# Last groups of a banded attention: GpSimd scales the probabilities, each turned tile is read by two engines, and the middle keys are turned once

## The chip, the core and the metric

The program runs on one core of a Trainium2 chip. The metric is the device time of one execution in microseconds (us), lower is better. One execution of each kernel was also taken by the hardware profiler; all rows come from it.

## What is computed

A decoder trunk of two layers, for 512 prompt tokens and 8 sample tokens. The change is in the token mixer of the second layer, attention of 16 heads (4 key heads) in blocks of 128 queries. Each query sees the block of keys before its own and its own block, within a band, and a learned sink takes part in the sum of each row:

```python
band = (diff >= 0) & (diff <= WINDOW)            # WINDOW = 128
s = jnp.where(mask[None, :, None, None], s, -jnp.inf)
p = sink_probs(s, sinks).astype(v.dtype)         # exp(s - mx) / (sum + exp(sink - mx))
o = jnp.einsum('bnkgqs,bnskd->bnqkgd', p, vc).reshape(B, T, SW_HEADS * SW_HD)
return o @ w_out, k[:, T - nkeep:], v[:, T - nkeep:]
```

## The kernel before

The program is written by hand: five instruction streams (TensorE, VectorE, ScalarE, GpSimd, SyncE) in a fixed order, which meet only at semaphores. An instruction that waits holds up all that stands behind it on its engine. Most of the time is dense products: a weight tile is split into a high and a low part (ScalarE writes `wH`, VectorE writes `wL`), and TensorE makes three products of each.

The attention is cut into 16 groups `gi` (4 sets of heads by 4 query blocks; `gi % 4 == 0` is the first block, which has no keys before it and so about two thirds of the work). Each group makes this round:

1. `window_scores(gi)`, TensorE: scores into the PSUM tile `tile`, four rows of 192 keys and a sink for each query.
2. `shift(gi)`, VectorE: minus the maximum of each row, into `sm`.
3. `exps(gi)`, ScalarE: four exponentials with their sums, into an SBUF buffer `soft`.
4. `normalise(gi)`, VectorE: reciprocal of the sums, then four multiplications, in place. The semaphore `s_norm` rises after the second and after the fourth.
5. `turn(gi)`, TensorE: transposes of 128 by 128 into the PSUM tile `side`, half 0 after the first rise of `s_norm`, half 1 after the second. In this buffer the two rows of a half are 257 wide with zeros where a row has no keys; the middle 128 keys of the two rows are turned one after the other and added up in PSUM, so that a half takes four transposes (two in a first block). GpSimd writes the zeros beforehand (`clear_between`).
6. `turn_read(gi)`: copy of `side` into SBUF `softT`. For groups 0 to 3 ScalarE reads half 0 and VectorE half 1, for groups 4 and 5 VectorE reads both, from group 6 on ScalarE reads both.
7. `weigh(gi)`, TensorE: turned probabilities by values, into `sums` (group 15: into `tile[0]`).
8. `att_high(gi)` on ScalarE and `att_low(gi)` on VectorE: the high and the low part of the result, `xH` and `xL`, which the output product `sout` reads.

Groups 0 to 4 run between the chunks of the product `qkv` (up to about 770 us of the trace), groups 5 to 15 without such cover, one behind the other (770 to 803 us). There TensorE's order is `window_scores(gi + 2)`, `turn(gi)`, `weigh(gi - 1)`; ScalarE's is `exps(gi + 1)`, `turn_read(gi)`, `att_high(gi - 1)`; VectorE's is `shift(gi + 1)`, `normalise(gi)`, `att_low(gi - 2)`. In group 7 VectorE also makes two products of the rotation of the last queries and in group 8 their sum (`rope_sum`), and in the last two groups TensorE makes `sample_scores` where `window_scores` would stand. Behind `weigh(15)` TensorE goes on with `sout`. TensorE waits before `window_scores(gi)` until `exps(gi - 2)` is done, before `turn(gi)` until `side` has been read, and before `weigh(gi)` until its turned tile has been copied.

## Time and profile before

| | |
|---|---|
| median of 3 runs | 1303.2 us (1303.16 to 1304.3) |
| profiled execution, its own time | 1304.2 us |
| its span in the trace | 1302.4 us |
| TensorE matmuls busy | 1290.9 us, 99% |
| VectorE / ScalarE / GpSimd busy | 888.9 / 593.4 / 73.7 us |
| granted TensorE clock, mean | 0.997 of full speed |

A row of the timeline gives the start, the time from the start of the first to the end of the last of its instructions, the engine, line, operation, output and inputs, the number of instructions, and in brackets the time that the engine stood idle before and what ended it. Ends of matmuls are modelled and overlap the next ones, so that the pace of TensorE is read from the distance between two starts.

### The profile page before, as it was taken

The numbers are of one execution on the slowest core, as the hardware profiler recorded it, in microseconds if no ns is written. First come the engines' busy times: TensorE is split into PE (matmuls) and PEld (weight loads), VectorE is DVE, ScalarE is ACT, GpSimd is POOL, SyncE is SP. The second block draws the span as 40 slices with busy tenths as digits, with TensorE's granted clock in tenths as the row PEclk, the third lists the DMA queues.
The fourth block names the chain that finished last, engine by engine and source line by source line (L and its number), as shares of the span: only waits on it lengthen the run. The fifth ranks groups of instructions, "written<-read, shape, count | busy, mean of one in ns | idle before, by whom it ended". The sixth has DMA issues, their size and how long they took to land.

```text
span 1302.4 us, 25274 instructions
## 1 busy us (share of the span) xinstructions
PE 1290.9 (99%) x10790; PEld 1257.8 (97%) x10790; DVE 888.9 (68%) x1597; ACT 593.4 (46%) x1059; POOL 73.7 (6%) x115
## 2 busy tenths in 40 slices
PE   9998999999999999999999999999999999999998
PEld 8998989999999999999999988999999999999998
DVE  7897876987777774223897787698777777422385
ACT  6213555544444442222754767555444444322371
POOL 1121330000000000000031010000000000000000
PEclk9998999999999999999999999999999999999999
DMA  5436622213323224221414232311323323322231
GB/s 199 155 97 189 227 81 82 91 42 97 96 83 98 94 92 135 90 90 62 146 51 151 77 98 80 98 66 49 98 82 98 95 85 110 113 90 92 77 129 66
DMA packets 35409, 131.84 MB, mean 101 GB/s; under 512 B 4469, under 2 KB 5085, under 8 KB 35009
## 3 DMA queue, kind: packets, MB, share of 16 engines
q1 hardware_dynamic: 29520, 111.33, 26.5%
q0 software_dynamic: 5344, 18.26, 4.3%
q8 instruction: 85, 1.39, 0.4%
q10 hardware_dynamic: 432, 0.64, 0.2%
q14 instruction: 28, 0.22, 0.1%
HBM read 121.26 MB, written 10.08 MB: 101 GB/s over the span
## 4 chain that ended last, share of the span: by engine, by line
PE 94%; DVE 2%; ACT 2%; DMA 1%; issue 0%; ACTq 0%; DVEq 0%
PE tile L1174 24%; PE tile L1176 24%; PE tile L1178 24%; PE tile L1184 4%; PE tile L1185 4%; PE tile L1186 4%; PE tile L1646 1%; PE side L1184 1%; DMA raw<-in_w_qo 1%; PE side L1185 1%; PE side L1186 1%; ACT xH L780 0%; DMA raw<-in_w_kv 0%; PE sums L1345 0%; DVE wL L1829 0%
## 5 line engine op out<-in xcount | busy, mean ns | idle before, releaser
L753 ACT ACTIVATE wH<-raw 128x1024 fp32r<-128x1024 f32 (+1 forms) x190 | 210.7, 1112 | 384.8 <-DMA raw<-in_w_up 145.6
L1174 PE MATMUL tile<-xH,wH 128*128 128x260 f32 x1798 | 363.7, 283 | 0.0
L1178 PE MATMUL tile<-xH,wL 128*128 128x260 f32 x1798 | 363.0, 284 | 0.0
L1176 PE MATMUL tile<-xL,wH 128*128 128x260 f32 x1798 | 362.6, 283 | 0.0
L1829 DVE TENSOR_TENSOR wL<-raw,wH 128x1024 fp32r<-128x1024 f32 (+1 forms) x190 | 245.8, 1295 | 159.7 <-ACT wH L753 155.6
L1174 PEld LDWEIGHTS tile<-xH,wH 128*128 128x128 f32 x1798 | 278.0, 189 | 3.9 <-issue 3.4
L1178 PEld LDWEIGHTS tile<-xH,wL 128*128 128x128 f32 x1798 | 278.0, 189 | 0.0
L1176 PEld LDWEIGHTS tile<-xL,wH 128*128 128x128 f32 x1798 | 277.4, 189 | 0.0
L1877 DVE SCALAR_TENSOR_TENSOR u<-tile,rstd 128x520 f32<-128x520 f32 x96 | 67.1, 699 | 121.7 <-PE tile L1178 121.6
L1174 PE MATMUL tile<-hidH,wH 128*128 128x260 f32 x616 | 124.3, 283 | 0.0
L1178 PE MATMUL tile<-hidH,wL 128*128 128x260 f32 x616 | 123.8, 282 | 0.0
L1176 PE MATMUL tile<-hidL,wH 128*128 128x260 f32 x616 | 123.8, 282 | 0.0
L1184 PE MATMUL tile<-xH,wH 128*128 128x260 f32 x400 | 116.0, 290 | 0.1
L1185 PE MATMUL tile<-xL,wH 128*128 128x260 f32 x400 | 113.1, 283 | 0.0
L1186 PE MATMUL tile<-xH,wL 128*128 128x260 f32 x400 | 112.8, 282 | 0.0
L1176 PEld LDWEIGHTS tile<-hidL,wH 128*128 128x128 f32 x616 | 95.1, 188 | 0.0
L1178 PEld LDWEIGHTS tile<-hidH,wL 128*128 128x128 f32 x616 | 94.9, 188 | 0.0
L1174 PEld LDWEIGHTS tile<-hidH,wH 128*128 128x128 f32 x616 | 94.8, 188 | 0.0
L1184 PEld LDWEIGHTS tile<-xH,wH 128*128 128x128 f32 x400 | 75.3, 188 | 2.7 <-issue 2.3
L1185 PEld LDWEIGHTS tile<-xL,wH 128*128 128x128 f32 x400 | 75.3, 188 | 0.3
L1186 PEld LDWEIGHTS tile<-xH,wL 128*128 128x128 f32 x400 | 75.3, 188 | 0.0
L974 ACT ACTIVATE cv<-u,taps 128x520 f32<-128x520 f32 x44 | 36.2, 823 | 48.8 <-DVE u L1877 48.4
(445 smaller groups left out, 1909.3 us busy)
## 6 DMA issues: line engine op xcount, KB each, us to landing
raw<-in_w_up SPq DMA_DIRECT2D x88, 512.0 KB, 3.6
raw<-in_w_down SPq DMA_DIRECT2D x32, 704.0 KB, 4.1
raw<-in_w_ple SPq DMA_DIRECT2D x16, 512.0 KB, 5.9
raw<-in_w_qo SPq DMA_DIRECT2D x12, 512.0 KB, 3.6
raw<-in_w_qkv SPq DMA_DIRECT2D x12, 512.0 KB, 3.6
raw<-in_w_kv SPq DMA_DIRECT2D x10, 512.0 KB, 3.7
cring<-in_c_in POOLq DMA_DIRECT2D x8, 512.0 KB, 4.7
out_c_s<-cring POOLq DMA_DIRECT2D x8, 512.0 KB, 3.2
```

The source lines that it names most:

```text
L753: nc.scalar.activation(wH[j][:, 0:n], raw[j][:, 0:n], ACT.Copy).then_inc(s_high, 1)
L974: nc.scalar.activation(dst[:], u[:, r, 2:], ACT.Identity, bias=taps[:, r, 3:4], scale=taps[:, r, 2:3]).then_inc(s_ca, 1)
L1174: nc.tensor.matmul(out[:, q, 0:HT], wh, x[0][:, k, tokens(q)], start=first, stop=False)
L1176: nc.tensor.matmul(out[:, q, 0:HT], wh, x[1][:, k, tokens(q)], start=False, stop=False)
L1178: mm = nc.tensor.matmul(out[:, q, 0:HT], wl, x[0][:, k, tokens(q)], start=False, stop=last)
L1184: nc.tensor.matmul(out, wh, x[0][:, k, tokens(q)], start=first, stop=False)
L1185: nc.tensor.matmul(out, wh, x[1][:, k, tokens(q)], start=False, stop=False)
L1186: return nc.tensor.matmul(out, wl, x[0][:, k, tokens(q)], start=False, stop=last)
L1646: nc.tensor.matmul(banks[half][:, e, at0 + 2 * HD - HD * m + k0:at0 + 3 * HD], queries[r, gp, m * P:m * P + P], qk[r, gp // 2, k0:HD * m + ...
L1829: nc.vector.tensor_tensor(wL[j][:, 0:n], raw[j][:, 0:n], wH[j][:, 0:n].bitcast(F32), ALU.subtract).then_inc(s_low, 1)
L1877: nc.vector.scalar_tensor_tensor(out=halves(dst), in0=bank(stage, c)[0:rows, :, 0:HT], scalar=scale, in1=halves(rstd[0:rows, :]), op0=ALU. ...
```

## The change

- The buffer `soft` loses the zeros between its two rows. The last 64 keys of the first row stand beside the first 64 of the second, so that three transposes turn a half (in a first block two, of which one is 64 columns wide). `clear_between` and its semaphore are gone. This holds for all 16 groups.
- From group 8 on (`SPREAD`) the four multiplications of `normalise` run on GpSimd (`scale`); VectorE keeps the reciprocal.
- From group 8 on ScalarE reads half 0 of the turned tile and VectorE half 1. `soft_late` has three places where it had two, and `exps` waits for the `turn` of three groups before, where it was two.

```diff
@@ -55,6 +55,7 @@
 BOTH = 6
+SPREAD = 8
 QUERIED = 6
@@ -277,13 +278,13 @@
         sw = Region(xH_at + KT // 2 * T * 4)
-        soft_early = sw("soft_early", [P, 2, 4, 2 * P + 1])
+        soft_early = sw("soft_early", [P, 2, 2, 2 * (3 * HD + 1)])
         assert sw.top <= xL_at
         sw = Region(xL_at + KT // 2 * T * 4)
         softT_early = sw("softT_early", [P, 2, 2, 3 * P])
         assert sw.top <= xL_at + KT * T * 4
         sw = Region(arena + size([P, KT, T]))
-        soft_late = sw("soft_late", [P, 2, 4, 2 * P + 1])
+        soft_late = sw("soft_late", [P, 3, 2, 2 * (3 * HD + 1)])
         softT_late = sw("softT_late", [P, 2, 2, 3 * P])
@@ -437,11 +439,24 @@
 
-            return (soft_early if gi < BESIDE else soft_late)[:, gi % 2]
+            return soft_early[:, gi % 2] if gi < BESIDE else soft_late[:, gi % 3]
+
+        def soft_row(gi, c):
+            at0 = c % 2 * (3 * HD + 1)
+            return soft_of(gi)[:, c // 2, at0:at0 + 3 * HD + 1]
 
         def softT_of(gi):
 
             return (softT_early if gi < BESIDE else softT_late)[:, gi % 2]
+
+        def scale(eng, gi):
+            lo = first_key(gi)
+            for c in range(4):
+                at0 = 1 if c % 2 == 0 and gi % 4 else 0
+                keys = soft_row(gi, c)[:, at0 + lo:at0 + 3 * HD]
+                step = eng.tensor_scalar(keys, keys, sm[:, gi % 2, 1, c:c + 1], None, ALU.mult)
+                if c % 2:
+                    step.then_inc(s_norm, 1)
 
@@ -467,7 +482,7 @@
         def both_on_act(gi):
-            return gi >= BOTH
+            return BOTH <= gi < SPREAD
 
@@ -475,6 +490,10 @@
             return gi + 1 - sum(both_on_dve(n) for n in range(gi + 1))
+
+        def turned_by_dve(gi):
+
+            return gi + 1 - sum(both_on_act(n) for n in range(gi + 1))
 
@@ -571,23 +590,16 @@
                     .to_broadcast([P, NQ // 2, 2, HD])))
-            clear_between(soft_early)
             assert made.n == MADE
 
         def last_rotation(pool):
             pool.wait_ge(s_mm, CHUNK0["qkv"] + COUNT["qkv"])
-            clear_between(soft_late)
             pool.wait_ge(s_read, READ0["qkv"] + LASTQ + 1)
             pool.wait_ge(s_rotr, LASTQ - 3)
             half = HD // 2
             for i in range(4):
                 pool.dma_start(rotated[half * i:half * i + half, LASTQ % 2, :],
                                u[half * (i ^ 1):half * (i ^ 1) + half, LASTQ % 2, 0:T]).then_inc(s_rotl, 16)
-
-        def clear_between(soft):
-            for e, column in enumerate((3 * HD + 1, 0)):
-                mm = nc.gpsimd.memset(soft[:].rearrange("p k (i e) t -> p (k i) e t", e=2)[:, :, e, column:column + HD], 0.0)
-            mm.then_inc(s_swk, 1)
 
@@ -735,6 +747,10 @@
                     nc.gpsimd.memset(acc[:], 0.0).then_inc(s_acc, 1)
+                    for gi in range(SPREAD, 4 * NB):
+                        pool.wait_ge(s_norm, 2 * gi)
+                        pool.wait_ge(s_inv, gi - SPREAD + 1)
+                        scale(nc.gpsimd, gi)
                     pool.wait_ge(s_rope, 2 + KT)
@@ -1099,12 +1115,14 @@
                 act.wait_ge(s_z, gi + 1)
-                if gi >= 2:
+                if 2 <= gi < BESIDE:
                     act.wait_ge(s_tu, 2 * (gi - 1))
+                if gi >= BESIDE + 3:
+                    act.wait_ge(s_tu, 2 * (gi - 2))
                 k = gi % 2
                 for c in range(4):
                     last = nc.scalar.activation(
-                        soft_of(gi)[:, c, w.start + HD * (c % 2):w.stop + HD * (c % 2)], score_tile(gi)[:, c // 2, :].rearrange("p (c s) -> p c s", c=2)[:, c % 2, w],
+                        soft_row(gi, c)[:, w], score_tile(gi)[:, c // 2, :].rearrange("p (c s) -> p c s", c=2)[:, c % 2, w],
                         ACT.Exp, bias=sm[:, k, 0, c:c + 1], accum_out=sm[:, k, 1, c:c + 1])
@@ -1662,30 +1680,23 @@
                     pe.wait_ge(s_tua, turned_by_act(gi - 1))
-                    pe.wait_ge(s_tud, min(gi, BOTH))
-                if gi == 0:
-                    pe.wait_ge(s_swk, 1)
-                if gi == BESIDE:
-                    pe.wait_ge(s_swk, 2)
+                    pe.wait_ge(s_tud, turned_by_dve(gi - 1))
                 soft = soft_of(gi)
                 for half in range(2):
                     pe.wait_ge(s_norm, 2 * gi + half + 1)
-                    earlier, later = soft[:, 2 * half, :], soft[:, 2 * half + 1, :]
-                    nc.tensor.transpose(side[:, half, 2 * P:3 * P], later[:, P:2 * P], ident)
                     if gi % 4 == 0:
-                        mm = nc.tensor.transpose(side[:, half, P:2 * P], earlier[:, P:2 * P], ident)
+                        mm = nc.tensor.transpose(side[0:HD, half, P:2 * P], soft[:, half, P:P + HD], ident)
                     else:
-                        nc.tensor.transpose(side[:, half, 0:P], earlier[:, 1:1 + P], ident)
-                        nc.tensor.matmul(side[:, half, P:2 * P], later[:, 0:P], ident, is_transpose=True,
-                                         start=True, stop=False, skip_group_check=True)
-                        mm = nc.tensor.matmul(side[:, half, P:2 * P], earlier[:, 1 + P:1 + 2 * P], ident, is_transpose=True,
-                                              start=False, stop=True, skip_group_check=True)
+                        for i in range(2):
+                            mm = nc.tensor.transpose(side[:, half, i * P:i * P + P], soft[:, half, 1 + i * P:1 + i * P + P],
+                                                     ident)
+                    mm = nc.tensor.transpose(side[:, half, 2 * P:3 * P], soft[:, half, 1 + 2 * P:1 + 3 * P], ident)
                     mm.then_inc(s_tu, 1)
 
             def weigh(gi):
                 gp, n = divmod(gi, 4)
                 pe.wait_ge(s_tua, turned_by_act(gi))
-                pe.wait_ge(s_tud, min(gi + 1, BOTH))
+                pe.wait_ge(s_tud, turned_by_dve(gi))
                 if 1 <= gi < 4 * NB - 1:
@@ -2509,16 +2520,13 @@
             def normalise(gi):
-                k = gi % 2
-                lo = first_key(gi)
                 dve.wait_ge(s_soft, gi + 1)
-                chain.link(nc.vector.reciprocal(sm[:, k, 1, :], sm[:, k, 1, :]))
-                for c in range(4):
-                    at0 = HD if c % 2 else 1 if gi % 4 else 0
-                    keys = soft_of(gi)[:, c, at0 + lo:at0 + 3 * HD]
-                    step = nc.vector.tensor_scalar(keys, keys, sm[:, k, 1, c:c + 1], None, ALU.mult)
-                    if c % 2:
-                        step.then_inc(s_norm, 1)
+                inverse = nc.vector.reciprocal(sm[:, gi % 2, 1, :], sm[:, gi % 2, 1, :])
+                if gi < SPREAD:
+                    chain.link(inverse)
+                    scale(nc.vector, gi)
+                else:
+                    inverse.then_inc(s_inv, 1)
 
@@ -2583,6 +2591,8 @@
                     normalise(gi)
+                if gi > SPREAD:
+                    turn_read(gi - 1)
                 if gi == BESIDE:
@@ -2598,6 +2608,7 @@
             att_low(groups - 2)
+            turn_read(groups - 1)
             att_low(groups - 1)
```

The program order shows where the new copy stands in VectorE's stream. These are VectorE's rows from the reciprocal of group 15 on, before: the multiplications, `att_low(13)`, the step for the samples, `wL`, then `att_low(14)` and `att_low(15)`.

```order
L2515 RECIPROCAL sm<-sm 128x4
L2519 TENSOR_SCALAR soft_late<-soft_late,sm 128x192 x4
L2535 TENSOR_TENSOR xL<-sums,xH 128x2x128
L2461 TENSOR_REDUCE sst<-tile 128x1
L2462 TENSOR_TENSOR sst<-sst 128x1
L2463 TENSOR_TENSOR sst<-sst 128x1
L1829 TENSOR_TENSOR wL_53<-raw_54,wH_52 128x1024
L2535 TENSOR_TENSOR xL<-sums,xH 128x2x128
L2535 TENSOR_TENSOR xL<-tile,xH 128x2x128
```

And the same place of the changed program, where the two copies of `side` are `turn_read(14)` and `turn_read(15)`:

```order
L2524 RECIPROCAL sm<-sm 128x4
L2537 COPY softT_late<-side 128x384
L2543 TENSOR_TENSOR xL<-sums,xH 128x2x128
L2472 TENSOR_REDUCE sst<-tile 128x1
L2473 TENSOR_TENSOR sst<-sst 128x1
L2474 TENSOR_TENSOR sst<-sst 128x1
L1840 TENSOR_TENSOR wL_53<-raw_54,wH_52 128x1024
L2543 TENSOR_TENSOR xL<-sums,xH 128x2x128
L2537 COPY softT_late<-side 128x384
L2543 TENSOR_TENSOR xL<-tile,xH 128x2x128
```

The copy of group 15's half 1 stands between the two last `att_low`, behind the one of group 14. On GpSimd, the rows between the rotation of the last queries and the first step of the next layer were these:

```order
L584 DMA rotated<-u 32x520 x4
L737 MEMSET acc 128x520
L739 MEMSET u 128x512
L713 DMA convw<-in_convw 128x176
L714 DMA prev<-in_conv_prev 128x704
```

They are now:

```order
L601 DMA rotated<-u 32x520 x4
L749 MEMSET acc 128x520
L457 TENSOR_SCALAR soft_late<-soft_late,sm 128x128 x4
L457 TENSOR_SCALAR soft_late<-soft_late,sm 128x192 x12
L457 TENSOR_SCALAR soft_late<-soft_late,sm 128x128 x4
L457 TENSOR_SCALAR soft_late<-soft_late,sm 128x192 x12
L755 MEMSET u 128x512
L725 DMA convw<-in_convw 128x176
L726 DMA prev<-in_conv_prev 128x704
```

The 32 multiplications of groups 8 to 15 stand ahead of a fill and of two loads for the next layer. On TensorE a first block (here group 0) was turned by four equal transposes:

```order
L1674 MATMUL side<-const,soft_early 128x128
L1676 MATMUL side<-const,soft_early 128x128
L1674 MATMUL side<-const,soft_early 128x128
L1676 MATMUL side<-const,soft_early 128x128
```

In the changed program every second one is 64 wide:

```order
L1688 MATMUL side<-const,soft_early 64x128
L1693 MATMUL side<-const,soft_early 128x128
L1688 MATMUL side<-const,soft_early 64x128
L1693 MATMUL side<-const,soft_early 128x128
```

Four transposes stay four here; in the twelve other groups eight become six.

## Rows read from the trace of the kernel before

**Rows 1.** The page: TensorE's busy time, and the chain that ended last.

```profile
PE 1290.9 (99%) x10790; PEld 1257.8 (97%) x10790; DVE 888.9 (68%) x1597; ACT 593.4 (46%) x1059; POOL 73.7 (6%) x115
...
PE 94%; DVE 2%; ACT 2%; DMA 1%; issue 0%; ACTq 0%; DVEq 0%
```

**Rows 2.** Windows, busy time of PE, PEld, DVE, ACT, POOL in five us.

```profile
785.00:790.00 5.00, 4.82 (x57) 3.57 (x56) 4.50 (x17) 5.00 (x22) 0.00 (x0) 1.00 0.15 58
```

**Rows 3.** Timeline of PE, one full round in the late groups.

```profile
788.60 0.92 PE L1646 MATMUL tile<-qk 64*128 64x192 f32 x8
...
789.69 0.27 PE L1674 MATMUL side<-const,soft_late 128*128 128x128 f32 x1
789.80 0.27 PE L1678 MATMUL side<-const,soft_late 128*128 128x128 f32 x1
...
790.66 0.44 PE L1697 MATMUL sums<-softT_late,vst 128*64 128x128 f32 x4
...
791.63 0.92 PE L1646 MATMUL tile<-qk 64*128 64x192 f32 x8
```

**Rows 4.** Timeline of PE, where it stood idle in the late groups.

```profile
773.66 0.44 PE L1697 MATMUL sums<-softT_late,vst 128*64 128x128 f32 x4 [0.24 <-issue]
...
780.92 0.30 PE L1674 MATMUL side<-const,soft_late 128*128 128x128 f32 x1 [0.21 <-DVE soft_late L2519]
...
785.83 0.71 PE L1646 MATMUL tile<-qk 64*128 64x64 f32 x8 [0.18 <-ACT soft_late L1106]
```

**Rows 5.** Timeline of PE, a `weigh` after dense products.

```profile
768.83 0.40 PE L1178 MATMUL tile<-pxH,wL 128*128 128x260 f32 x2
769.16 0.44 PE L1697 MATMUL sums<-softT_early,vst 128*64 128x128 f32 x4
```

**Rows 6.** Timeline of POOL, the only multiplications by a scalar column.

```profile
679.62 2.92 POOL L563 TENSOR_SCALAR partsB<-partsB,sinks 128x8 bf16<-128x8 bf16 x3
```

**Rows 7.** Timeline of DVE in the same stretch.

```profile
681.00 0.76 DVE L2349 SCALAR_TENSOR_TENSOR pxL<-h,front,pxH 128x520 fp32r<-128x520 f32 x1 [0.19 <-ACT pxH L1058]
681.67 0.69 DVE L2342 TENSOR_TENSOR cv<-gate_more,pwo 128x520 f32<-128x520 f32 x1
```

**Rows 8.** POOL by source line: shortest, median and longest ns.

```profile
L563 POOL TENSOR_SCALAR partsB<-partsB,sinks x3: 598/852/1284, 679.6 to 681.9; 128x8 bf16<-128x8 bf16 x3
...
L571 POOL CAST bandB<-const x2: 1041/1393/1745, 699.1 to 700.8; 128x1024 bf16<-128x1024 f32 x2
...
L609 POOL TENSOR_TENSOR prob<-prob,kvq x4: 997/1010/1023, 140.5 to 179.2; 128x384 f32<-128x384 f32 x4
```

**Rows 9.** Timeline of DVE, the steps of groups 8 and 15.

```profile
780.09 0.17 DVE L2515 RECIPROCAL sm<-sm 128x4 f32<-128x4 f32 x1
...
781.49 0.68 DVE L2421 TENSOR_TENSOR qk<-cg,cv 128x512 f32<-128x512 f32 x1
...
799.16 0.18 DVE L2515 RECIPROCAL sm<-sm 128x4 f32<-128x4 f32 x1 [1.19 <-ACT soft_late L1106]
799.37 1.01 DVE L2519 TENSOR_SCALAR soft_late<-soft_late,sm 128x192 f32<-128x192 f32 x4
```

**Rows 10.** Timeline of PE, the end of the attention.

```profile
800.16 0.33 PE L1674 MATMUL side<-const,soft_late 128*128 128x128 f32 x1
...
801.18 0.44 PE L1697 MATMUL sums<-softT_late,vst 128*64 128x128 f32 x4
...
802.15 0.44 PE L1697 MATMUL tile<-softT_late,vst 128*64 128x128 f32 x4
...
803.12 0.39 PE L1184 MATMUL tile<-xH,wH 128*128 128x260 f32 x1
```

**Rows 11.** Timeline of ACT, the end of the attention.

```profile
802.29 0.38 ACT L1124 ACTIVATE xH<-sums 128x256 fp32r<-128x256 f32 x1 [0.18 <-PE sums L1708]
```

**Rows 12.** Timeline of DVE, its last steps, and an early half copy.

```profile
761.29 0.55 DVE L2529 COPY softT_early<-side 128x384 f32<-128x384 f32 x1
...
802.70 0.42 DVE L2535 TENSOR_TENSOR xL<-sums,xH 128x256 fp32r<-128x256 f32 x1 [0.27 <-ACT xH L1124]
```

5 lines of the change are left out of this document (3 added, 2 removed).

## The prediction

> **What bounds the kernel now.** I read the page first. TensorE is busy 99% of the span and the chain that ended last lies on it for 94% [rows 1]: whatever is taken off TensorE's stream counts at once, unless TensorE then waits for something else, and a wait that it did not have before counts in full. GpSimd has nothing to do for 94% of the time.
>
> Then the windows of the late groups. From 785 to 790 us TensorE and ScalarE both show 5.00 of 5 us, VectorE 4.50 [rows 2]. So there are three nearly full engines, and a round of a group passes through all of them.
>
> Then TensorE's timeline. One full round runs from 788.60 to 791.63, 3.03 us: scores 1.09, `turn` 0.97 (from 789.69 to 790.66), `weigh` 0.97. The transposes start 0.11 us apart (789.69, 789.80), though each shows 0.27 [rows 3]: the price of a transpose is 0.11. The stream does not run without gaps. It stood before `weigh(5)` (for VectorE's copy), before `turn(8)` (for VectorE's multiplications) and before `window_scores(12)` (for ScalarE's exponentials of group 10) [rows 4]. At these three places a transpose saved ahead of the gap only makes the gap longer.
>
> **The change part by part.**
>
> Transposes. 24 of them go (12 groups, one in each half), 24 x 0.11 = 2.64 us. In groups 1, 2 and 3 dense products stand around them and TensorE waits for nothing: 6 x 0.11 = -0.66. Group 5's two are lost in the gap before `weigh(5)`, those of 6 and 7 in the gap before `turn(8)`, those of 9 in the gap before `window_scores(12)` [rows 4]. Left are groups 10, 11, 13, 14 and 15, each -0.22, if GpSimd keeps up (below).
>
> The 64-wide transpose. No row of before has one. The nearest: between two dense products of `qkv` TensorE goes on every 0.12 us, so the pair at 768.83 should be followed at 769.07; `weigh`, whose weights are 64 wide, starts at 769.16 [rows 5], 0.09 later. In a first block the widths now go 128, 64, 128, 64, 128, four changes where there was none. Below: nothing, as the load of a narrow tile might be free when the output is a transpose. Above: 0.09 for each of four, 0.36 a group. I take 0.3, as every `weigh` shows the gap: groups 0, 4 and 12, +0.9; in group 8 it lies in a wait. The Trainium skill has a rule here, in TensorEngine Tiling, Key Properties: changing the tiling mode drains TensorE. By it all four changes cost, as by the row; without it the sum would be 0.9 lower.
>
> GpSimd's multiplication. VectorE takes 1.01 us for its four (799.37) [rows 9], about 0.24 each. GpSimd's price is the term that decides most. Its only multiplications by a scalar column are three of 8 elements, and they took 598 to 1284 ns, 2.92 us together [rows 6, 8]. Taken as a fixed cost this would be about 0.97 each. But at the same time VectorE ran instructions with two inputs in SBUF: one from 681.00 to 681.76, the next from 681.67 to 682.36 [rows 7], and GpSimd's last one ended at 682.54, 0.18 behind it. I read the three as blocked by VectorE, and not as slow. A conversion of 1024 elements with one input took 1.04 us at its best [rows 8], so 1.0 ns an element at most; 192 elements give 0.20, and with about 0.1 for the start 0.30. Below: 0.20, that rate with no start. Above: the product of two tensors of 384 elements took 1.01 us [rows 8], 2.6 ns an element, so 0.50; above that again the 0.97 of the three. I take 0.30, from the row that has one input as these have. The Trainium skill's GPSIMD Engine Reference says in Key points that VectorE is about twice as fast in elementwise work; by that the price would be near 0.5 and the sum that of the slow rival below. No row here shows it for one input.
>
> What GpSimd's price does. `turn(gi)` starts when the first two products are there and its second half when all four are. Two products take 0.6, TensorE's half of a `turn` now takes 0.37: where TensorE stands right behind GpSimd, its second half waits 0.22, just what the two transposes saved.
> - Group 8. The reciprocal is at 780.09 [rows 9], GpSimd starts near 780.3, and its four short products (128 elements, 0.2 each) are ready at 781.1 if nothing blocks them. But VectorE's `rope_sum`, two inputs in SBUF, 0.68 us (781.49 before) [rows 9], is now due near 780.4, since the four products no longer stand ahead of it. It and the third product collide, and `turn(8)` ends up to 0.6 later. `weigh(7)` started right behind `turn(8)` before. Bounds -0.1 and +0.7; I take +0.2, as half the products are through by then.
> - Group 10 follows the wait for ScalarE at 785.83 [rows 4]: behind `exps(10)` come one score step on TensorE (0.84) and, beside it, reciprocal, hop, two products, hop: 0.1 + 0.15 + 0.6 + 0.2 = 1.05, and the second half after that. TensorE stands behind GpSimd; +0.1.
> - Group 11: -0.2. Group 13: -0.2.
> - Groups 14 and 15. The stream of TensorE holds less here. For 15 the reciprocal came at 799.16 [rows 9] and `turn` at 800.16 [rows 10]; 799.16 + 1.05 = 800.2. So what was gained before is lost here, and the second half waits: together +0.2.
>
> The copy of group 15. This is the term I am surest of. Before, `weigh(15)` started at 802.15, at once behind `weigh(14)` [rows 10]. Now it needs `turn_read(15)` of VectorE, which stands behind `att_low(14)`, which needs `att_high(14)` of ScalarE, which needs the end of `weigh(14)`. The times of this chain are in the rows: `weigh(14)` ends at 802.15, `att_high(14)` starts at 802.29 [rows 11], `att_low(14)` at 802.70 [rows 12] and gives way 0.33 later, at 803.03; the copy of half a turned tile takes 0.55 (761.29) [rows 12], to 803.58; 0.1 of hop. `weigh(15)` starts at 803.68 in place of 802.15: +1.5. Behind it stands all of `sout`, whose first product was at 803.12 [rows 10], on the same engine. Nothing covers it. ScalarE's shorter copy and the third place of `soft_late` cannot help here; elsewhere they take off load from ScalarE, which is full [rows 2], and I give them no price, as TensorE's waits are for GpSimd then.
>
> The other moves on GpSimd, the fill for the samples and two loads, go from 783 us to after 801. They are used only within and after `sout`: +0. The removed zero fills: 0, nothing waited for them.
>
> Sum: -0.66 + 0.9 + 0.2 + 0.1 - 0.2 - 0.2 + 0.2 + 1.5 = +1.8 (group 12 is in the 0.9). On the profiled execution's own 1304.2 this gives 1306.0, its span 1302.4 becoming 1304.2; that execution was 1.0 above the median of the runs, 1303.2, on which I predict: 1305.0 us.
>
> **The rivals.**
>
> *Faster.* If the narrow transpose is free, GpSimd needs 0.2 or less and `rope_sum` does not collide, TensorE is the bound throughout: -2.64 + 0.22 (group 5) + 1.5 = -0.9, and the gaps before `turn(8)` and `window_scores(12)` close, -0.4: 1301.9. For it speaks that VectorE and ScalarE are both relieved; against it that ScalarE's exponentials, not its copies, set the pace of group 10, and that GpSimd's rate in the rows gives 0.20 only with no start. To pass 0.2% the copy of group 15 would have to be hidden as well, and the order of the stream excludes that.
>
> *Slower, GpSimd as the bound.* At 0.36 to 0.40 for a product the second halves start to wait in every group, since two products are then longer than the 0.37 and the round's slack is used up. At 0.5 the second half of `turn` waits 0.6 in groups 10, 14 and 15 and some 0.2 to 0.6 in the others; walking the round through with 0.5 I get +4.5 in place of +1.8, 1307.7. At 0.97 GpSimd's 3.9 us a group against a round of 2.8 rules all eight: about +18, 1321. For it speak the three rows taken at their face; against, the match of their ends with VectorE's.
>
> *Slower, the lock.* The Trainium skill says the same of two-input instructions, in SBUF — State Buffer, Who interferes with whom. The trace agrees in the three rows. As a mechanism of this kernel it strikes once, in group 8, at +0.7 rather than +0.2: 1305.5.
>
> **How the numbers follow.** My forecast, with the lock in group 8 either way, 1303.7 to 1306.4: 0.52. The faster rival with its milder forms, 1301 to 1303.7: 0.15. GpSimd between 0.36 and 0.6, 1306.4 to 1311: 0.27. GpSimd near 0.97: 0.06. The range takes in the first three but for their tails: 1302.3 to 1308.8. A measurement of this kernel can tell about 0.2%, 2.6 us, from no change, so "slower" begins at 1305.8: all of the slow cases and a tenth of mine, 0.33 + 0.05 = 0.38. "Faster" ends at 1300.6: 0.04. The rest, 0.58, is no change that can be told.
>
> **What the new profile would show.** Right: `weigh(15)` idle for some 1.5 us behind `weigh(14)`, released by VectorE's copy; GpSimd's products about 0.3 us apart; a gap of near 0.1 at each narrow transpose; the second half of `turn` behind GpSimd in groups 10, 14 and 15. Wrong: products 0.5 apart or more (slow rival), `turn(8)` no later than before (no collision), or narrow transposes 0.11 apart on both sides (that term is nothing).

## The result, and the profile after

The changed kernel takes 1317.3 us (median of 4 runs, 1316.35 to 1318.12), the kernel before 1303.4 beside it (1303.16 to 1304.3). The ratio is 1.0104, with a 95% interval of 1.0092 to 1.0116: by it the kernel is 13.6 us slower (the two medians lie 14.0 apart). The forecast of 1305.0 had foreseen 1.8 us, and its range ended at 1308.8.

The page of the changed kernel, the lines that answer to [rows 1]:

```profile
PE 1294.0 (98%) x10766; PEld 1257.1 (96%) x10766; DVE 886.0 (67%) x1573; ACT 592.2 (45%) x1059; POOL 95.6 (7%) x143
...
PE 90%; DVE 4%; ACT 2%; POOL 2%; DMA 1%; issue 1%; ACTq 0%; DVEq 0%; POOLq 0%
```

TensorE's share of the chain that ended last fell from 94% to 90%, and GpSimd is now in it. GpSimd's own timeline shows why:

```profile
779.65 2.55 POOL L457 TENSOR_SCALAR soft_late<-soft_late,sm 128x128 f32<-128x128 f32 x4 [7.06 <-DVE sm L2524]
783.51 2.99 POOL L457 TENSOR_SCALAR soft_late<-soft_late,sm 128x192 f32<-128x192 f32 x4 [1.31 <-DVE sm L2524]
787.82 2.99 POOL L457 TENSOR_SCALAR soft_late<-soft_late,sm 128x192 f32<-128x192 f32 x4 [1.31 <-DVE sm L2524]
...
804.26 6.08 POOL L457 TENSOR_SCALAR soft_late<-soft_late,sm 128x192 f32<-128x192 f32 x8 [1.31 <-DVE sm L2524]
```

Four products of a full group take 2.99 us, 0.75 each, where I had taken 0.30 and VectorE needed 1.01 for all four [rows 9]. And GpSimd then stands idle for 1.31 us before it may begin the next group, so that two scalings start 4.31 us apart (783.51 to 787.82), against a round of 3.03 before [rows 3]. It waits for the reciprocal of VectorE, and VectorE's timeline says what that waited for:

```profile
786.61 0.96 DVE L2518 TENSOR_REDUCE sm<-tile 128x4 f32<-128x772 f32 x1 [1.61 <-POOL soft_late L457]
787.49 0.17 DVE L2524 RECIPROCAL sm<-sm 128x4 f32<-128x4 f32 x1
787.57 0.53 DVE L2537 COPY softT_late<-side 128x384 f32<-128x384 f32 x1
```

GpSimd ends group 9 at 783.51 + 2.99 = 786.50; `shift(11)` starts at 786.61, `reciprocal(10)` behind it in VectorE's order at 787.49, GpSimd's group 10 at 787.82. The list of waits in the late groups (us in total, times, the longest) names the two halves of this ring. Of the first, 7.1 us lie ahead of GpSimd's first group and do not belong to it:

```profile
POOL soft_late L457 <- DVE sm L2524: 14.8, 7, 7.1
...
DVE sm L2518 <- POOL soft_late L457: 10.1, 6, 2.1
```

`shift(gi + 1)` waits for `s_norm` of group `gi - 1`. Before, VectorE had raised that semaphore itself, and the wait was over when it came to it. Now it is GpSimd's, the reciprocal of group `gi` stands behind it, and GpSimd's next scaling needs that reciprocal: scaling, `shift`, reciprocal, scaling, and none of these steps overlaps another.

TensorE's timeline shows the waits, where [rows 4] had three of 0.18 to 0.24:

```profile
781.18 0.27 PE L1688 MATMUL side<-const,soft_late 128*64 128x128 f32 x1 [1.37 <-POOL soft_late L457]
782.25 0.30 PE L1688 MATMUL side<-const,soft_late 128*64 128x128 f32 x1 [0.69 <-POOL soft_late L457]
...
790.87 0.44 PE L1691 MATMUL side<-const,soft_late 128*128 128x128 f32 x2 [0.87 <-POOL soft_late L457]
...
812.31 0.70 PE L1708 MATMUL sums<-softT_late,vst 128*64 128x128 f32 x4
...
815.44 0.44 PE L1708 MATMUL tile<-softT_late,vst 128*64 128x128 f32 x4 [1.53 <-DVE softT_late L2537]
...
816.41 0.39 PE L1202 MATMUL tile<-xH,wH 128*128 128x260 f32 x1
```

And its windows (the window's length, then the busy time of PE, PEld, DVE, ACT and POOL in it, then TensorE's granted clock). The first five are five us long, the last two lie inside them and are one us long:

```profile
780.00:785.00 5.00, 3.12 (x26) 2.10 (x28) 2.33 (x5) 2.36 (x9) 3.69 (x7) 0.79 0.00 0
785.00:790.00 5.00, 4.29 (x37) 2.66 (x33) 2.53 (x7) 4.48 (x19) 3.69 (x6) 0.87 0.02 5
790.00:795.00 5.00, 3.22 (x32) 1.98 (x32) 1.74 (x4) 2.73 (x11) 3.80 (x6) 1.00 0.00 0
...
805.00:810.00 5.00, 3.22 (x26) 2.02 (x30) 0.91 (x3) 1.86 (x10) 4.91 (x8) 0.68 0.00 0
810.00:815.00 5.00, 3.92 (x38) 2.58 (x33) 2.76 (x7) 1.22 (x3) 2.02 (x5) 0.64 0.33 90
...
784.00:785.00 1.00, 1.00 (x10) 0.98 (x8) 0.42 (x1) 0.84 (x2) 1.00 (x3) 0.50 0.00 0
...
808.00:809.00 1.00, 1.00 (x9) 0.72 (x8) 0.56 (x1) 0.00 (x0) 1.00 (x3) 0.50 0.00 0
```

Where [rows 2] had three engines nearly full, VectorE is now busy about half the time, and at two places the granted clock fell to 0.50, the lower level of 1.2 GHz, after TensorE had stood still.

To compare single executions I use the stage from the first transpose of group 0 to the first product of `sout`: before 733.35 to 803.12 [rows 10], 69.77 us; changed 733.36 to 816.41, 83.05 us. The stage holds +13.28 us, nearly all of the difference. What lies behind the stage, to the end of the span, takes 499.2 to 499.3 us in the profiled execution of every kernel here but two (e2 and f7, below), so that the stage says nearly all there is to say.

### The profile page after: what moved, and what is told of

Read it like the earlier page. It is cut to its first block, busy times and chain, and to the rows that moved or that the text cites. A ratio compares the mean times of both kernels' runs of the same rounds, so it can differ in the third digit from the quotient of the medians.

```text
span 1315.7 us, 25241 instructions
## 1 busy us (share of the span) xinstructions
PE 1294.0 (98%) x10766; PEld 1257.1 (96%) x10766; DVE 886.0 (67%) x1573; ACT 592.2 (45%) x1059; POOL 95.6 (7%) x143
## 4 chain that ended last, share of the span: by engine, by line
PE 90%; DVE 4%; ACT 2%; POOL 2%; DMA 1%; issue 1%; ACTq 0%; DVEq 0%; POOLq 0%
PE tile L1192 23%; PE tile L1196 23%; PE tile L1194 23%; PE tile L1202 4%; PE tile L1203 4%; PE tile L1204 4%; POOL soft_late L457 2%; DMA raw<-in_w_qo 1%; DVE wL L1840 1%; PE side L1202 1%; PE side L1203 1%; PE side L1204 1%; PE tile L1664 1%; ACT xH L796 0%; DVE cv L1873 0%
```

## Experiments

Times are medians. The ratio is to the kernel before on the same chip in the same job; the medians of the kernel before lie between 1303.1 and 1303.9 in these jobs, so kernels of different jobs are compared by their ratios. "Stage" is the stretch defined above, in us, from one execution.

| kernel | us | ratio and interval | stage |
|---|---|---|---|
| changed | 1317.32 | 1.0104, 1.0092 to 1.0116 | 83.05 |
| e1: VectorE scales | 1304.9 | 1.0010, 1.0000 to 1.0019 | 71.63 |
| e2: ring opened | 1312.08 | 1.0069, 1.0056 to 1.0083 | 78.11 |
| e3: turned once only | 1302.05 | 0.9989, 0.9980 to 0.9998 | 68.03 |
| e4: copy of 15 earlier | 1315.1 | 1.0090, 1.0076 to 1.0104 | 81.24 |
| f1: filler on TensorE | 1314.35 | 1.0090, 1.0076 to 1.0103 | 80.91 |
| f4: price list on e3 | 1303.69 (1 run) | | 69.49 |
| f5: e3, group 5 on ScalarE | 1301.3 | 0.9990, 0.9981 to 0.9998 | 68.14 |
| f6: half on each engine | 1304.15 | 1.0009, 1.0000 to 1.0018 | 70.65 |
| f7: product of two tensors | 1308.17 | 1.0039, 1.0025 to 1.0052 | 73.51 |
| f8: f7, ring opened, copy early | 1305.82 | 1.0020, 1.0011 to 1.0029 | 72.56 |
| f9: copies alone | 1304.07 | 1.0004, 0.9995 to 1.0013 | 70.88 |
| g1: f8 without shared copies | 1306.18 | 1.0019, 1.0010 to 1.0028 | 72.03 |

### The three parts apart

**e1**, the change with the scaling put back on VectorE:

```diff
-                    for gi in range(SPREAD, 4 * NB):
-                        pool.wait_ge(s_norm, 2 * gi)
-                        pool.wait_ge(s_inv, gi - SPREAD + 1)
-                        scale(nc.gpsimd, gi)
...
-                if gi < SPREAD:
-                    chain.link(inverse)
-                    scale(nc.vector, gi)
-                else:
-                    inverse.then_inc(s_inv, 1)
+                chain.link(inverse)
+                scale(nc.vector, gi)
```

> The changed kernel with one part undone: VectorE makes the four multiplications of all 16 groups again, GpSimd none; the shared reading of the turned tile, the three places of soft_late and the transposes stay as changed. Theory A (GpSimd's multiplications, 0.75 us each, make up nearly all of the loss; at the end remains the copy of group 15, 1.5 us): +0.5 to +2.5 us on the kernel before, 1304 to 1306, and no window of the late groups with a lower granted clock. Rival B (the loss is in the split reading and in the narrow transposes): above +6.

Measured 1304.9, granted clock 1.00 in all windows. The stage is 11.42 us shorter than the changed kernel's: GpSimd's scaling, with all that it brings, is that much of the 13.28. The waits that stay are for VectorE's copy, in TensorE's timeline:

```profile
783.76 0.41 PE L1687 MATMUL side<-const,soft_late 128*128 128x128 f32 x2 [0.76 <-DVE softT_late L2530]
...
804.05 0.44 PE L1704 MATMUL tile<-softT_late,vst 128*64 128x128 f32 x4 [1.52 <-DVE softT_late L2530]
```

**e2**, the ring opened; GpSimd scales as in the change:

```diff
@@ exps(gi)
+                if gi >= 2:
+                    act.wait_ge(s_norm, 2 * (gi - 1))
@@ shift(gi)
-                    dve.wait_ge(s_norm, 2 * (gi - 1))
+                    dve.wait_ge(s_soft, gi - 1)
```

> The changed kernel; VectorE's row maximum (shift) of a group no longer waits until the group two before has been scaled, ScalarE's exponentials wait for that instead (they are what overwrites the sums). GpSimd's work is the same. Theory A1 (the round of 4.3 us is a ring: GpSimd's scaling 3.0, then shift 0.9 and reciprocal on VectorE, then the next scaling, so that GpSimd stands idle 1.3 us in each group): the idle time of GpSimd goes, the distance of two groups' scalings falls from 4.3 to 3.1 to 3.9 us, and the time falls by 3 to 7 us, to 1310 to 1314. Rival A2 (GpSimd's price alone sets the round): no more than 1 us less, 1316 to 1318.

1312.08, the stage 4.94 us shorter. GpSimd's timeline now has scalings much closer to each other:

```profile
796.02 2.98 POOL L457 TENSOR_SCALAR soft_late<-soft_late,sm 128x192 f32<-128x192 f32 x4 [0.74 <-DVE sm L2526]
799.15 2.98 POOL L457 TENSOR_SCALAR soft_late<-soft_late,sm 128x192 f32<-128x192 f32 x4 [0.15 <-POOL soft_late L457]
```

799.15 - 796.02 is 3.13 us, GpSimd's own price and little more. Not all of GpSimd's idle time went: between its first and its last scaling it is 4.4 us in place of 7.7, and the longest that is left is this one:

```profile
785.95 6.05 POOL L457 TENSOR_SCALAR soft_late<-soft_late,sm 128x192 f32<-128x192 f32 x8 [2.00 <-DVE sm L2526]
```

From the first scaling's start to the last one's it takes 24.41 us (778.34 to 802.75), in the changed kernel 27.7 (779.65 to 807.3, halfway through the row of eight). So the ring itself is worth 3.3 us of the 4.94. Another 1.5 lie behind the last scaling, where the changed kernel's clock was low. In e2 it fell later: the windows from 809 to 812 us show 0.56, 0.50 and 0.50, `sout` starts within them at 810.26, and what lies behind the stage takes 500.3 us, 1.1 more than elsewhere. The ring is real, and it is less than half of what GpSimd costs.

**e3**, the kernel before with the middle keys turned once (the edit is to the changed kernel). The three places of `soft_late`, and the looser wait of `exps` that goes with them, do not depend on `SPREAD` and stay in:

```diff
-SPREAD = 8
+SPREAD = 16
...
-            turn_read(groups - 1)
```

> The kernel before with only the packed buffer and its transposes (24 fewer, and 8 narrow ones): VectorE scales everywhere, ScalarE reads both halves from group 6 on. Theory C (a transpose is 0.11 us on TensorE, a narrow one costs as a wide one, and five late groups as well as three early ones are bound by TensorE): -1.0 to -2.3 us, 1301.0 to 1302.4. Rival D (ScalarE sets the round of the late groups, so that a saved transpose is waited for there): -0.3 to -0.9 us, from the early groups alone.

1302.05, faster than the changed kernel and, by 0.1% with an interval that stays below 1, than the one before. The stage is 1.74 us shorter than before. Whether the third place has any part in that is not shown; the transposes alone were predicted to give 1.76 (below).

**e4**, the two last copies exchanged:

```diff
-            att_low(groups - 2)
             turn_read(groups - 1)
+            att_low(groups - 2)
             att_low(groups - 1)
```

> The changed kernel with VectorE's copy of group 15 moved ahead of att_low(14). Theory E (weigh(15) waits 1.5 us for that copy alone, and all of sout stands behind it): 1.2 to 1.6 us less than the changed kernel, 1315.7 to 1316.2, and weigh(15) starts right behind weigh(14). Rival F (the weights of sout or the granted clock hold the end): the wait moves to the first products of sout, under 0.4 us less.

1315.1, by the ratios 1.8 us less than the changed kernel and so a little more than the 1.2 to 1.6 that were expected. TensorE's row of `weigh(15)` shows no wait any more, and the stage is 1.81 us shorter.

**f9**, e1 with the exchange of e4. It differs from e3 by the shared copies alone, since e3 has the third place too (against what was written down before the run):

> VectorE scales all groups, the middle keys are turned once, each turned tile from group 8 on is read half by ScalarE and half by VectorE, three places, and group 15's is read ahead of att_low(14). So it differs from the kernel with the middle keys turned once only by the shared copies and the third place. Theory (ScalarE's load was not what TensorE waited for, so that sharing the copy is worth nothing, and VectorE, 4.50 of 5 us busy, pays for it): 1302.3 to 1304, 0 to 2 us behind the 1302.05 of the kernel with the middle keys turned once only. Rival (sharing pays once its tail is gone): below 1301.5, and this would be the version to keep.

1304.07, 2.0 us behind e3 by the ratios, the stage 2.85 behind. Most of it is that `turn(gi + 1)` has to wait until VectorE has read its half, and that copy stands behind VectorE's four products. VectorE's and then TensorE's timeline:

```profile
784.00 1.01 DVE L457 TENSOR_SCALAR soft_late<-soft_late,sm 128x192 f32<-128x192 f32 x4
784.93 0.55 DVE L2530 COPY softT_late<-side 128x384 f32<-128x384 f32 x1
```

```profile
785.58 0.41 PE L1687 MATMUL side<-const,soft_late 128*128 128x128 f32 x2 [0.38 <-issue]
```

The row says "issue", but the copy ends at 785.48, 0.10 before the transpose starts. The tail is not gone either. Ahead of the copy of group 15 now stands VectorE's `wL`, and `weigh(15)` still waits 0.76 us. VectorE's rows and TensorE's:

```profile
800.40 1.22 DVE L1836 TENSOR_TENSOR wL<-raw,wH 128x1024 fp32r<-128x1024 f32 x1
801.53 0.55 DVE L2530 COPY softT_late<-side 128x384 f32<-128x384 f32 x1
```

```profile
802.23 0.44 PE L1704 MATMUL tile<-softT_late,vst 128*64 128x128 f32 x4 [0.76 <-DVE softT_late L2530]
```

So the exchange that gave 1.81 us in the changed kernel gives 0.75 here (stages of e1 and f9).

### The price of a GpSimd multiplication

**f4**, on e3, in a stretch where GpSimd has nothing else to do:

```diff
+                    tried = Chain(pool, sem("tried"))
+                    for n in (8, 64, 192, 288):
+                        for _ in range(3):
+                            tried.link(nc.gpsimd.tensor_scalar(scratch[:, 0:n], const[:, 0:n], eps[:, 0:1], None, ALU.mult))
...
+                            tried.link(nc.gpsimd.tensor_scalar(scratch[:, 0:n], const[:, 0:n], 2.0, None, ALU.mult))
...
+                            tried.link(nc.gpsimd.tensor_copy(scratch[:, 0:n], const[:, 0:n]))
...
+                        tried.link(nc.gpsimd.tensor_tensor(scratch[:, 0:192], const[:, 0:192], const[:, 0:192], ALU.mult))
```

> A price list, on the kernel with the middle keys turned once and nothing else changed. GpSimd makes 30 instructions on a scratch tile in a stretch where it has nothing else to do, each behind the one before: three each of a multiplication by a column for 8, 64, 192 and 288 elements a row, by a constant for 8 and 192, a copy of 8 and of 192, a product of two tensors of 192. Theory B (the price belongs to the instruction): the multiplication by a column costs 0.29 us and 2.5 ns an element, so 0.31, 0.45, 0.77 and 1.01 us. Theory D (the start is dear, and the size counts little): the three before the change, 598 to 1284 ns for 8 elements, were the true price, so all sizes near 0.6 to 0.9. For the kind: if the column is what costs, the constant takes 0.3 us or less at 192 and the copy about 0.3 (1 ns an element, as the conversions of 1024 elements in 1.04 us before the change); if all operations of this width run at one rate, constant and copy also take 0.7 to 0.8. The product of two tensors: 0.78 (2.6 ns an element plus the start). The time of the kernel should be that of its base, 1302 +- 1, as nothing waits for these.

The groups by shape (busy us, mean ns of one, idle us before), and one instruction each of the two larger column sizes from GpSimd's timeline:

```profile
L754 POOL TENSOR_SCALAR scratch<-const,eps 128x8 f32<-128x8 f32 x3 | 0.9, 311 | 0.2
...
L757 POOL TENSOR_SCALAR scratch<-const 128x192 f32<-128x192 f32 x3 | 2.2, 733 | 0.2
...
L760 POOL COPY scratch<-const 128x192 f32<-128x192 f32 x3 | 1.0, 342 | 0.2
...
L762 POOL TENSOR_TENSOR scratch<-const 128x192 f32<-128x192 f32 x3 | 1.5, 506 | 0.2
```

```profile
775.22 0.76 POOL L754 TENSOR_SCALAR scratch<-const,eps 128x192 f32<-128x192 f32 x1
...
780.65 1.00 POOL L754 TENSOR_SCALAR scratch<-const,eps 128x288 f32<-128x288 f32 x1
```

The shortest of three each, 0.31, 0.76 and 1.00 for 8, 192 and 288 elements, lie on 0.29 us and 2.5 ns an element, as expected. With 64 the shortest was 0.44, which fits too. VectorE worked beside them, and some took longer: one of 192 took 0.87 (776.08), one of 288 took 1.52 (777.90). A constant is hardly cheaper than a column (0.69 at its best); a copy of the same size takes 0.34, close to my 0.30; and what I had not expected, the product of two tensors takes 0.51 and is cheaper than the product with one. The kernel's time was to stay that of e3; the one run and the stage (+1.46) say that it did not. The likely cause is in VectorE's rows. Its four products took 1.01 us in e3 and up to 1.43 beside GpSimd, and TensorE waited for them three times before a `turn` (0.61, 0.26 and 0.19 us), in e3 once (0.32):

```profile
788.66 1.43 DVE L458 TENSOR_SCALAR soft_late<-soft_late,sm 128x192 f32<-128x192 f32 x4
```

**f7**, the change with the other form on GpSimd:

```diff
+                    step = eng.tensor_tensor(keys, keys, inverse.to_broadcast([P, 3 * HD - lo]), ALU.mult)
```

> The changed kernel, but GpSimd scales with a product of two tensors, the second being the column of inverse sums repeated along the row, in place of the multiplication by a column. In the price list a GpSimd product of two tensors of 192 took 0.51 us, the multiplication by a column 0.76 for the same 192. Theory P (the form sets GpSimd's price, and the price and the ring set the loss): four products take 2.05 us in place of 2.99, the distance of two scalings falls from 4.3 us by 0.94 to 3.36 (idle of GpSimd still 1.3), and seven rounds give 6 to 6.6 us back, less where TensorE's own round of 2.8 takes over: 1311 to 1312.5. Rival Q (a repeated column is no cheaper than the column form): the four take 2.8 us or more and the time stays at 1316 to 1318. Rival R (two inputs in SBUF collide with VectorE's att_low and rope work and slow both): four take 2.3 to 2.6 and VectorE's two-input rows grow, 1313 to 1315.5.

1308.17, 3 us better than the best that was expected. GpSimd's timeline:

```profile
788.37 1.89 POOL L461 TENSOR_TENSOR soft_late<-soft_late,sm 128x192 f32<-128x192 f32 x4 [1.15 <-DVE sm L2528]
791.56 1.47 POOL L461 TENSOR_TENSOR soft_late<-soft_late,sm 128x128 f32<-128x128 f32 x4 [1.29 <-DVE sm L2528]
```

The mechanism of theory P holds: four products 1.89 instead of 2.99, starts 3.19 apart, GpSimd's idle time nearly as it was. From the first scaling to the last it took 21.42 us (778.54 to 799.96), in the changed kernel 27.7 (779.65 to 807.3, halfway through the row of eight): 6.2 us less, as expected. Of the 9.54 us by which the stage is shorter the rest was left out of the expectation: the last scaling counts too (1.1), and the clock stayed at 1.00 from 775 to 805 us (2.1 by f1). But it fell right behind the stage, where `sout` had started at 805.90:

```profile
805.00:810.00 5.00, 5.00 (x37) 4.66 (x38) 2.37 (x6) 1.07 (x5) 0.00 (x0) 0.66 0.67 240
```

What lies behind the stage takes 500.9 us here, 1.6 more than elsewhere. So most of what the stage saved on the clock was paid later, and the whole kernel is 8.5 us faster than the changed one by the ratios.

**f8** is f7 with the edits of e2 and e4.

> The same, and with it the ring opened (shift waits for the exponentials of two groups before, the exponentials wait for the scaled probabilities) and group 15's turned tile read ahead of att_low(14). GpSimd's 2.05 us a group is then below the round of 2.8 us, and nothing of VectorE waits for it. Theory: what is left is latency, two products of 1.0 us before each half of turn where VectorE needed 0.5, so up to 0.5 us a group where TensorE stands right behind; 1303 to 1307. By my prediction's walk with 0.5 us a product the kernel would be at 1307.7 with the copy of group 15 unhidden, 1306.1 with it hidden. Rival S (GpSimd's work itself, by slowing VectorE and ScalarE or by one more hop in the chain of each group, costs what the price list does not show): 1308 or more.

1305.82, inside the expected range and 2.6 us over before by the ratio. TensorE's waits name what is left: 2.5 us in all for GpSimd's scaling (1.46 of them in group 8, then 0.19 to 0.32 in four groups) and 0.39 before `weigh(15)` for VectorE's copy. That is the latency of a slower engine in the chain of each group; between its groups GpSimd itself stands idle again.

**f6**, the dose between: VectorE scales rows 0 and 1, GpSimd rows 2 and 3 beside it, with a semaphore of its own, and the edits of e2 and e4:

```diff
+                    dve.wait_ge(s_inv, gi - SPREAD + 1)
+                    scale(nc.vector, gi, (0, 1))
...
-                        scale(nc.gpsimd, gi)
+                        scale(nc.gpsimd, gi, (2, 3))
```

> The dose between none and four GpSimd products a group. From group 8 on VectorE scales rows 0 and 1 and GpSimd rows 2 and 3, beside each other behind the same reciprocal, with a semaphore of its own for GpSimd's half; shift waits for the exponentials of two groups before in place of the scaled probabilities, and group 15's turned tile is read ahead of att_low(14). Theory (GpSimd's 0.75 us a product and the ring are the whole loss): two products take 1.5 us, well below the round of 2.8 us, so GpSimd bounds nothing; the first half of turn starts as in the kernel before, the second 0.9 us after it in place of 0.37, so up to 0.5 us a group where TensorE stands right behind, less where it has slack. With the copy of group 15 costing nearly nothing now: 1302.5 to 1305.5. Rival (any GpSimd work there slows VectorE through SBUF, VectorE being busy 4.50 of 5 us): VectorE's multiplications and att_low get longer by 20% or more, and the time is 1307 or more.

1304.15, as the theory had it, and the first half of the rival is true as well. The two engines slow each other: VectorE's two products take 0.72 (four took 1.01 alone, so two about 0.5), GpSimd's two 1.63 (1.52 by the price list):

```profile
795.28 0.72 DVE L463 TENSOR_SCALAR soft_late<-soft_late,sm 128x192 f32<-128x192 f32 x2
```

`att_low` did not get longer (0.41), and the time stayed 3 us below the rival's. Against f9, which differs by the scaling and its waits, f6 is the same within its interval.

**g1** has f8's scaling, and ScalarE reads the whole turned tile as before the change:

```diff
-SPREAD = 8
+SPREAD = 16
+GPS = 8
...
-                    for gi in range(SPREAD, 4 * NB):
+                    for gi in range(GPS, 4 * NB):
...
-            turn_read(groups - 1)
```

> Middle keys turned once; from group 8 on GpSimd scales with the product of two tensors, the ring is open, three places; but the turned tiles are read whole by ScalarE, as before the change, so no copy of VectorE stands in any round from group 6 on. It differs from the kernel with two-input form and open ring (1305.8) by the shared copies alone, and from the one with the middle keys turned once only (1302.05) by GpSimd's scaling alone. Theory (the shared copy costs some 2 us wherever it is, since VectorE's half stands behind other work and the next turn waits for it): 1303 to 1304.3, and GpSimd's scaling itself costs 1 to 2 us by its latency. Rival U (with VectorE relieved of its multiplications the shared copy is no longer late there, so sharing costs nothing and ScalarE's whole copy now waits instead): 1305 to 1306.5. Rival V (with VectorE relieved and ScalarE's order unchanged this is the best form): below 1301.5.

1306.18 against f8's 1305.82, stages 72.03 and 72.56: rival U, with the median inside its range and the interval's reach of 1 us around it. Where VectorE no longer multiplies, its half of the copy is not late in the rounds; sharing costs nothing there that the runs can tell and brings nothing. The stages differ by 0.53, of which 0.39 is f8's wait before `weigh(15)`. So the price of sharing depends on what VectorE has ahead of the copy.

### The clock

**f1**, products that nobody reads, in front of TensorE's waits:

```diff
                 for half in range(2):
+                    for _ in range(0 if gi < SPREAD else 3 if half else {8: 5, 10: 3, 13: 1, 14: 4}.get(gi, 0)):
+                        nc.tensor.matmul(side[:, half, 3 * P:4 * P], ones, ident, start=True, stop=True)
```

> Question: how much of the changed kernel's loss is TensorE's clock? In its trace the granted clock is 0.79 and 0.87 of full speed from 780 to 790 us and 0.68 and 0.64 from 805 to 815 us, stretches in which TensorE stood waiting before; elsewhere it is 1.00. This kernel is the changed one with products of ones by the unit matrix put in front of TensorE's waits (three ahead of the second half of each turn from group 8 on, five ahead of the first half in group 8, three in group 10, one in 13, four in 14), written to columns of side that nobody reads; they use up time in which TensorE stood. Theory F (the clock is the rest): walking the late groups through with 0.75 us for a GpSimd product gave +11.2 of the +13.3 us between the first transpose and the first product of sout, and the early transposes -0.6, so that some 2.6 us are left for the clock. Then the granted clock is 1.00 or near it in these windows, turn and window_scores take 1.1 us there in place of 1.5 to 2.0, and the time falls by 1.5 to 2.8 us against the changed kernel, to 1314.5 to 1315.8. Rival G (the slow TensorE instructions were hidden in the wait for GpSimd): the clock rises and the time stays within 0.6 us, 1316.7 to 1317.9, since the round is GpSimd's 3.0 us and the 1.3 us between its groups. Rival H: the filler stands in the way, each product of it behind an unfinished wait, and the time rises by 1 us or more.

1314.35, 1.8 us less than the changed kernel by the ratios; the stage is 2.14 us shorter. Windows of f1 at the two places:

```profile
780.00:785.00 5.00, 4.40 (x43) 3.03 (x43) 1.84 (x5) 2.83 (x10) 3.69 (x6) 1.00 0.01 2
...
805.00:810.00 5.00, 4.73 (x58) 3.74 (x58) 1.88 (x7) 2.19 (x8) 4.91 (x8) 1.00 0.00 0
```

GpSimd's timeline of f1 tells where the time came from:

```profile
779.15 2.55 POOL L457 TENSOR_SCALAR soft_late<-soft_late,sm 128x128 f32<-128x128 f32 x4 [7.07 <-DVE sm L2526]
...
803.75 6.07 POOL L457 TENSOR_SCALAR soft_late<-soft_late,sm 128x192 f32<-128x192 f32 x8 [1.31 <-DVE sm L2526]
```

From the first to the last start it is 24.60 us, in the changed kernel 24.61 (779.65 to 804.26). The slow clock from 780 to 790 us cost nothing: there the ring set the pace (rival G, for this place). Behind the start of that last row, to `sout`, it is 10.13 us (813.88 - 803.75) against 12.15: nearly all of theory F's gain lies there, where TensorE is the last in the chain again.

### A gap elsewhere

**f5**, on e3: group 5's turned tile read by ScalarE.

```diff
-            return BOTH <= gi < SPREAD
+            return BESIDE <= gi < SPREAD
...
-            return BESIDE - 1 <= gi < BOTH
+            return BESIDE - 1 <= gi < BESIDE
```

> On the kernel with the middle keys turned once and nothing else changed (1302.05): group 5's turned tile is read whole by ScalarE, ahead of its exponentials of group 6, in place of VectorE. Theory (the gap of 0.46 us before weigh(5) was VectorE's queue: shift and normalise stand ahead of its copy): the gap closes and the time falls by 0.3 to 0.6 us. Rival: the exponentials of group 6 start later by the copy's 0.6 us and the gap before turn(8) grows by as much; within 0.2 us of its base. Either is near what the measurement can tell; the traces' gaps decide.

The gap before `weigh(5)` went and another of 0.45 came before `window_scores(8)`, which waits for the exponentials of group 6, now behind the copy. The stage is 0.11 longer than e3's, and the two intervals are nearly the same. The rival is right, with its wait one step earlier than it said (the one before `turn(8)` grew by 0.10).

## Why the prediction was wrong

**What bounds the kernel now** held: what was taken off TensorE counts (e3), and a wait that it did not have counts in full. One reading was wrong. In [rows 2] the first 5.00 is the length of the window, and TensorE's busy time is 4.82; no term of the sum hangs on it.

**GpSimd's multiplication: the step that failed.** The prediction took 0.30 us; the runs show 0.75 for 192 elements and 0.59 for 128 at their shortest (2.99 and 2.35 us for four). I reasoned from the row that had as many inputs, a conversion. It predicts the copy (0.34) and not the multiplication. The bound "above" of 0.50, from the product of two tensors, was no bound either: that form takes 0.51 for 192, and the one with a column 0.25 more. The three rows of 8 elements were probably read rightly as lengthened by VectorE: in f4 such a product takes 0.31, and 0.6 to 1.3 stood in [rows 8]. (Those are bf16 and f4's float32; no run has the bf16 ones without VectorE beside them.) The mistake was to throw away their lower end with the rest, and with it a start of 0.3 that I set at 0.1. Nothing in my chances stood between 0.6 and 0.97, where the price turned out to be.

**What GpSimd's price does: right in kind.** The point from which it decides was given as 0.36 to 0.40 a product, and the walk as +4.5 at 0.5 and +18 at 0.97; on the line between, 0.75 gives +11.7, where +13.3 was measured in the stage. f7, with 0.47 a product, came to 1308.2 where the walk gave 1307.7 for 0.5. Both agreements are luck in part: the walk knows neither the ring nor the clock, and its +18 does not follow from the prediction's own terms, since 3.9 us against a round of 2.8 in eight groups is 8.8, and 10.6 with the +1.8.

**The ring: left out.** The prediction asked what stands behind GpSimd on TensorE, and not what stands behind it on VectorE. With four products of 0.30 the ring would have had 1.2 + 1.31 = 2.5 us (an estimate from these rows), less than a round, and been harmless; at 2.99 it costs 3.3 us between GpSimd's first and last scaling (e2).

**The clock: left out.** 2.1 us (f1), a result of the waits. In f7 and e2 a low clock behind the stage cost another 1.6 and 1.1 us.

**The copy of group 15: right.** +1.5 predicted; 1.53 in the changed kernel, 1.52 in e1, and 1.8 us of the stage given back by e4 (0.75 where VectorE scales, since a wait of 0.76 stays there, f9). The chain was as walked: `att_low(14)` at 814.41, the copy at 814.75 with 0.55, `weigh(15)` at 815.44.

**ScalarE's relief had "no price": wrong where VectorE multiplies.** Sharing cost 2.0 us with VectorE's products ahead of it (f9 against e3), and nothing that the runs can tell with those on GpSimd (g1 against f8).

**Transposes: right in size, the narrow ones wrong.** In the changed kernel's timeline of TensorE four transposes of group 4, narrow and wide in turn, start as densely as wide ones, and the dense product behind them 0.03 after the last:

```profile
766.62 0.27 PE L1688 MATMUL side<-const,soft_early 128*64 128x128 f32 x1
766.73 0.27 PE L1693 MATMUL side<-const,soft_early 128*128 128x128 f32 x1
766.84 0.27 PE L1688 MATMUL side<-const,soft_early 128*64 128x128 f32 x1
766.94 0.27 PE L1693 MATMUL side<-const,soft_early 128*128 128x128 f32 x1
766.97 0.37 PE L1192 MATMUL tile<-pxH,wH 128*128 128x260 f32 x1
```

So the +0.9 was nothing. The rule of the Trainium skill's TensorEngine Tiling (Array Packing), Key Properties, a drain at each change of mode, does not show in these rows, though it may in the 0.09 before each `weigh` [rows 5]. Groups 1 to 3 saved 0.6 us by the start of `turn(5)` (770.62 against 771.20). Of the whole 2.64, e3 kept 1.74, where the prediction had 0.66 and five times 0.22, 1.76; its gap before `weigh(5)` grew from 0.24 to 0.46 by just the two transposes, as the prediction said.

**The collision in group 8** was there and small: the first four products took 2.55 in place of the 2.35 of the other short group. What TensorE waited there, 1.37 and 0.69, is the price of the products again.

Taken together, in the stage: turned once -1.74 (e3); shared copies and the copy of 15 +3.60 (e1 less e3); GpSimd's scaling +11.42 (the changed kernel less e1), in which the ring is 3.3 and the clock 2.1. (e2's 4.9 and f1's 2.1 may not be added, since both count the stretch behind the last scaling.) What is left, some 6 us, I put down to GpSimd's own pace of 3.0 us a group and its latency; f7 and f8, which shorten the products, show the direction, but no run takes it apart further.

The best kernel of the study is e3; f5 is the same within what the runs can tell.

## What to carry to other kernels

Price an instruction on GpSimd by its own kind: here a copy, a product with a column and a product of two tensors of one size took 0.34, 0.76 and 0.51 us, so the number of inputs is no guide. When a step moves to another engine, list every wait on its semaphore, on all engines, and walk once round each loop that it closes; a wait that was always over because the same engine had raised the semaphore is the one to look for. And try the parts of a change apart: one of three was worth keeping, and the other two hid it. Where a stage is compared and not the whole, look behind its end as well: in f7 1.6 us of a slow clock lay just past it.

## What the runs showed of the hardware

- A GpSimd multiplication by a column costs 0.29 us and 2.5 ns an element; as a product of two tensors with the column repeated, the same work in the kernel took 0.47 us (1.89 for four) in place of 0.75.
- GpSimd and VectorE slowed each other also when VectorE's instruction had one input in SBUF: its four products took 1.10 to 1.43 us beside GpSimd's work (f4) and 1.01 alone, two 0.72 (f6). The Trainium skill has this in SBUF — State Buffer, Who interferes with whom, for VectorE's faster modes, and says that the later instruction is blocked fully. The rows show lengthening by a tenth to two fifths, 0.42 us at most for four products, where one GpSimd product alone takes 0.76.
- TensorE's granted clock fell to 1.2 GHz after waits of 1.4 and 0.7 us within one group (781.18, 782.25), and f1, which kept it busy there, had 1.00 throughout. After the waits of 0.70 and 0.87 in group 10 (789.47, 790.87) it did not fall. A wait of 1.5 us before `weigh(15)` was followed by 0.66 in f7 and by 1.00 in e1. The low clock cost time only where TensorE was last in the chain: nothing between 780 and 790 us of the changed kernel, 2.0 us behind its last scalings, 1.6 us in f7's `sout`.
